# Gate pieces as three rounded products, and ScalarE taking the gate selection and the inner row rounding of the expert turns

## What is computed

```
# mixer: the gates of the merge are a projection of h, 3 x 1024 columns wide
g_merge = (h @ w_in + b_in)[:, -3 * 1024:]
gm = sigmoid(g_merge.reshape(B, S, 3, 1024))
merged = gm[:, :, 0] * (o_a @ w_branch[0]) + gm[:, :, 1] * (o_b @ w_branch[1]) + gm[:, :, 2] * (o_c @ w_branch[2])

# experts: each token goes to 4 of 32, weighted by the softmax of their logits
gate = softmax(top_v)
hb = xb @ w1[e] + b1[e];  g, u = hb[:, :1024], hb[:, 1024:]
g = minimum(g, 7.0);  u = clip(u, -7.0, 7.0)
y = ((u + 1.0) * g * sigmoid(1.702 * g)) @ w2[e] + b2[e]
out = zeros.at[row_tok].add(y * row_w[:, None])
```

## Time and profile before

| | |
|---|---|
| median of three runs | 2846.25 us (2841.96 to 2849.76) |
| profiled execution, its own time | 2838.52 us |
| its span | 2836.7 us |
| TensorE busy | 2732.5 us, 96% |
| VectorE busy | 2101.5 us, 74% |
| ScalarE busy | 1516.0 us, 53% |
| read from HBM | 773 MB, 273 GB/s over the span |

### The profile page before, as it was taken

One profiled execution on the slowest core, in us unless ns is written; L12 is line 12 of the kernel. 1 busy time (PEld: TensorE's weight loads), 2 busy tenths in 40 slices (PEclk: granted clock), 3 DMA queues, 4 the chain that ended last, 5 costly groups with the idle time before them and its releaser, 6 DMA issues. The chain is left out here.

```text
span 2836.7 us, 43415 instructions
## 1 busy us (share of the span) xinstructions
PE 2732.5 (96%) x17490; PEld 2458.2 (87%) x17490; DVE 2101.5 (74%) x1854; ACT 1516.0 (53%) x1296; POOL 0.4 (0%) x6
## 2 busy tenths in 40 slices
PE   6999999999999999999998999999989999999998
PEld 5888888877787877778776999999979999999998
DVE  6335549999999999999998888676446766754453
ACT  0033318888888888888884443343444444432342
POOL 0000000000000000000000000000000000000000
PEclk9999999999999999999998999999999999999999
DMA  9753438999999999999995876777417767754551
GB/s 392 262 178 126 153 125 354 378 369 381 382 383 385 381 385 383 383 383 385 364 382 209 282 271 248 252 255 258 156 60 252 276 224 260 273 171 164 163 188 66
DMA packets 172689, 776.08 MB, mean 274 GB/s; under 512 B 12272, under 2 KB 38000, under 8 KB 121616
## 3 DMA queue, kind: packets, MB, share of 16 engines
q1 hardware_dynamic: 168640, 768.71, 71.5%
q10 hardware_dynamic: 3920, 5.49, 0.7%
HBM read 773.10 MB, written 1.05 MB: 273 GB/s over the span
## 5 line engine op out<-in xcount | busy, mean ns | idle before, releaser
L2271 DVE TENSOR_TENSOR w_low<-ring,w_high 128x2048 fp32r<-128x2048 f32 x396 | 880.6, 2285 | 16.3 <-DVE arena L2322 7.1
L901 ACT ACTIVATE w_high<-ring 128x2048 fp32r<-128x2048 f32 x396 | 734.6, 1906 | 75.4 <-PE psum L1564 75.3
L2411 DVE TENSOR_TENSOR w_low<-ring,w_high 128x2048 fp32r<-128x2048 f32 (+1 forms) x199 | 432.8, 2184 | 326.9 <-ACT w_high L1019 324.0
L1019 ACT ACTIVATE w_high<-ring 128x2048 fp32r<-128x2048 f32 (+1 forms) x199 | 362.4, 1829 | 567.6 <-PE psum L1204 489.2
L1204 PE MATMUL psum<-h_high,w_high 128*128 128x256 f32 x2080 | 591.4, 284 | 21.6 <-ACT h_high L1032 20.2
L1204 PE MATMUL psum<-h_high,w_low 128*128 128x256 f32 x2080 | 593.5, 285 | 0.0
L1204 PE MATMUL psum<-h_low,w_high 128*128 128x256 f32 x2080 | 591.1, 286 | 0.0
L1204 PEld LDWEIGHTS psum<-h_high,w_high 128*128 128x128 f32 x2080 | 402.7, 194 | 23.9 <-issue 22.1
L1204 PEld LDWEIGHTS psum<-h_low,w_high 128*128 128x128 f32 x2080 | 397.7, 192 | 0.0
L1204 PEld LDWEIGHTS psum<-h_high,w_low 128*128 128x128 f32 x2080 | 396.7, 191 | 0.0
L1564 PE MATMUL psum<-w_low,xg 128*128 128x512 f32 x1056 | 294.4, 400 | 4.1 <-DVE w_low L2271 2.9
(11 more groups left out here) (278 smaller groups left out, 3226.3 us busy)
## 6 DMA issues: line engine op xcount, KB each, us to landing
ring<-in_exp_w SPq DMA_DIRECT2D x396, 1024.0 KB, 8.3
ring<-in_ffn_w SPq DMA_DIRECT2D x135, 1024.0 KB, 5.2
ring<-in_mod_w SPq DMA_DIRECT2D x96, 1024.0 KB, 5.6
ring<-in_ffn_w SPq DMA_DIRECT2D x40, 768.0 KB, 4.8
ring<-in_w_in SPq DMA_DIRECT2D x24, 1024.0 KB, 10.7
ring<-in_even_w_in SPq DMA_DIRECT2D x12, 1024.0 KB, 7.2
ring<-in_conv_w_in SPq DMA_DIRECT2D x12, 1024.0 KB, 5.1
ring<-in_w_branch SPq DMA_DIRECT2D x6, 1024.0 KB, 5.1
```

The source lines that it names most:

```text
L901: act.activation(high_ap(j, D), slot_ap(PLAN.moe_slot + j), ACT.Copy).then_inc(sem("expert_high_ready" + c.x), 1)
L1019: act.activation(high_ap(m, cols), slot_ap(s, 2, cols), ACT.Copy).then_inc(sem("w_high_ready"), 1)
L2271: dve.tensor_tensor(low_ap(PLAN.moe_slot + j, D), slot_ap(PLAN.moe_slot + j), high_ap(j, D).bitcast(F32), ALU.subtract).then_inc(sem("expe ...
L2411: dve.tensor_tensor(low_ap(s, cols), slot_ap(s, 2, cols), high_ap(m, cols).bitcast(F32), ALU.subtract).then_inc(sem("w_split"), 1)
```

## The change

Three things change.

1. **Gate pieces.** Each of the twelve pieces is made of three products of split operands (`split_piece`). ScalarE rounds h once (`h1_high`, in the arena) and each piece's weights (`high_piece`, into ring places 7 and 8 in turn); VectorE makes the low part of h in place over `hT`, behind the last z piece, and each piece's low part in place over its slot (`low_piece`). Piece n+1 is prepared in step s of piece n: on ScalarE behind the exponentials of step s+1, on VectorE behind step s's modulation slots. The ring has seven places instead of nine from there to the experts; two small buffers move into ring place 11.
2. **Gate selection.** `selG` is made by ScalarE (`gated`): four activations of 128 x (2 x 64) with a scale read per partition, ahead of (first pair) or behind the copy of gather half 0. `select` on VectorE keeps only the comparison, without a wait, and signals `sel_ready` behind it.
3. **Inner rows.** The rounding of the inner rows is done by ScalarE (`hidden_rounded`): of expert 0 behind high part 17, of expert 1 behind the row copy of the down product of expert 0. VectorE issues the hidden product without waiting, does one low part in between (slot 16, or slot 20), waits for the rounding, and subtracts.

```diff
+            act.activation(h1_high[:, :, :], hT[:, :, :], ACT.Copy).then_inc(sem("h1_high_ready"), 1)
@@ ScalarE, attention steps
+            def high_piece(n):
+                s = PLAN.slots[f"mpiece{n}"]
+                if n < 2:
+                    await_release(act, PLAN.piece_before[n])
+                else:
+                    await_unit(act, U[f"mpiece{n - 2}"])
+                await_slot(act, s)
+                act.activation(piece_parts(n)[0], slot_ap(s, DC, 2 * P), ACT.Copy).then_inc(sem("piece_high_ready"), 1)
+            high_piece(0)
             for s in range(len(ATT)):
                 turned(s)
                 if s + 1 < len(ATT):
                     exps(s + 1)
+                if s in PIECE_STEPS and s != PIECE_STEPS[-1]:
+                    high_piece(PIECE_STEPS.index(s) + 1)
@@ ScalarE, expert turns
+            def gated(gate_of):
+                for b in range(TB):
+                    for e in range(2):
+                        chosen = sel[:, b, e, :].bitcast(F32)[:, None, :].broadcast_to([P, 2, CAP])
+                        act.activation(selG[:, b, e, :, :], chosen, ACT.Copy, scale=gate_of(580 + COLS_E * b + e))
+                def hidden_rounded(e):
+                    act.wait_ge(sem("hidden_whole" + c.x), c.turn * 2 + (e + 1))
+                    act.activation(hid[e][:, :, 0, :], moe_buf("up").rearrange("p (k s) -> p k s", k=DC),
+                                   ACT.Copy).then_inc(sem("hidden_high" + c.x), 1)
-                high(c, 15, 16, 17, 18)
+                high(c, 15, 16, 17)
+                hidden_rounded(0)
+                high(c, 18)
...
                 rows("down0", "y_rows0", 1.0 / ALPHA)
+                hidden_rounded(1)
                 c.await_unit(act, "gather0")
                 gathered(0, c.unit("gather0"), c.x)
+                gated(lambda at: small[:, bass.ds(c.columns + (at + 2), 1)])
                 high(c, 23)
@@ TensorE
+            def split_piece(n):
+                ...
+                pe.wait_ge(sem("piece_split"), n + 1)
+                wh, wl = piece_parts(n)
+                for k in range(DC):
+                    for j in range(2):
+                        dst, cols = unit(u)[:, j * T:(j + 1) * T], slice(j * P, (j + 1) * P)
+                        pe.matmul(dst, wh[:, k, cols], h1_high[:, k, :], start=(k == 0 and j == 0), stop=False, ...)
+                        pe.matmul(dst, wh[:, k, cols], h_low[:, k, :], start=False, stop=False, ...)
+                        mm = pe.matmul(dst, wl[:, k, cols], h1_high[:, k, :], start=False, stop=(k == DC - 1), ...)
@@ VectorE, attention steps
+            await_unit(dve, U["zpiece3"])
+            dve.wait_ge(sem("h1_high_ready"), 1)
+            dve.tensor_tensor(h_low[:, :, :], hT[:, :, :], h1_high[:, :, :].bitcast(F32), ALU.subtract)...
+            low_piece(0)
             soft(1)
...
                 for i in range(*ATT_MOD_SLOTS[s:s + 2]):
                     mod_slot(20 + i)
+                if s in PIECE_STEPS and s != PIECE_STEPS[-1]:
+                    low_piece(PIECE_STEPS.index(s) + 1)
                 if s == SUBLN_STEP:
                     subln_mean()
                 if s == SUBLN_STEP + 2:
                     subln_scale()
@@ VectorE, expert turns
-                    steps.link(dve.scalar_tensor_tensor(ub, ub, 1.0, glu, ALU.add, ALU.mult))
-                    steps.link(dve.tensor_scalar(hid[e][:, :, 0, :], ub, 1.0, None, ALU.mult))
+                    dve.scalar_tensor_tensor(ub, ub, 1.0, glu, ALU.add, ALU.mult).then_inc(sem("hidden_whole" + c.x), 1)
+                    low(c, *between)
+                    dve.wait_ge(sem("hidden_high" + c.x), c.turn * 2 + (e + 1))
                     dve.tensor_tensor(hid[e][:, :, 1, :], ub, hid[e][:, :, 0, :].bitcast(F32), ALU.subtract)...
-                up_half(0)
-                low(c, 16, 17, 18)
+                up_half(0, 16)
+                low(c, 17, 18)
...
-                up_half(1)
-                low(c, 20, 21, 22, 23)
+                up_half(1, 20)
+                low(c, 21, 22, 23)
```

More of the change, by code:

```diff
@@ L41 @@
 Z_PIECES = [8, 10, 12, 14]
-RING, RING1 = 12, 9
+RING, RING1, RING_ATT = 12, 9, 7
 SLOT = 2 * D
@@ L238, in make_plan @@
     p.piece("zpiece3", 14)
+    p.placed()
+    p.piece_before = [p.holder[at] for at in range(RING_ATT, RING1)]
+    p.places, p.next = RING_ATT, p.next % RING_ATT
     p.unit("cmp_turn", 2)
@@ L272, in make_plan @@
     p.placed()
+    for n in (10, 11):
+        p.holder[RING_ATT + n % 2] = p.slots[f"mpiece{n}"]
     p.high_before = [p.holder[at] for at in range(RING2, RING1)]
@@ L471, in build @@
         cmpP = area(14336, TB * 8, 16)
-        cmpPT, hidden_rows = area(11264, 2048), area(11264, 2, 2 * P)
+        cmpPT = ring[:, RING - 1, :]
+        hidden_rows = ring[:, RING - 1, 0:4 * P].rearrange("p (m c) -> p m c", m=2)
         gm = ring[:, RING1:RING, :].rearrange("p s (c t) -> p (s c) t", t=T)
@@ L981, in _ @@
                 await_unit(act, U["gather"] + half)
+                if half == 0:
+                    gated(first_gate)
                 gathered(half, unit(U["gather"] + half), "")
@@ L1454, in compressed @@
                 mm.then_inc(psum_full, 1)
+            def split_piece(n):
+                u = U[f"mpiece{n}"]
+                open_unit(pe, u)
+                if n == 0:
+                    pe.wait_ge(sem("h1_low_ready"), 1)
+                pe.wait_ge(sem("piece_split"), n + 1)
[3 more added lines that the diff above has]
+                        dst, cols = unit(u)[:, j * T:(j + 1) * T], slice(j * P, (j + 1) * P)
+                        pe.matmul(dst, wh[:, k, cols], h1_high[:, k, :], start=(k == 0 and j == 0), stop=False,
+                                  skip_group_check=True)
+                        pe.matmul(dst, wh[:, k, cols], h_low[:, k, :], start=False, stop=False, skip_group_check=True)
+                        mm = pe.matmul(dst, wl[:, k, cols], h1_high[:, k, :], start=False, stop=(k == DC - 1),
+                                       skip_group_check=True)
+                mm.then_inc(psum_full, 1)
             for n in range(len(Z_PIECES)):
@@ L1465, in _ @@
                 if s in PIECE_STEPS:
-                    piece(f"mpiece{PIECE_STEPS.index(s)}")
+                    split_piece(PIECE_STEPS.index(s))
                 if s:
@@ L2039, in _, with low_piece @@
             last.then_inc(sem("cmp_probs"), 1)
+            def low_piece(n):
+                s = PLAN.slots[f"mpiece{n}"]
+                dve.wait_ge(sem("piece_high_ready"), n + 1)
+                high, low_ = piece_parts(n)
+                dve.tensor_tensor(low_, slot_ap(s, DC, 2 * P), high.bitcast(F32), ALU.subtract).then_inc(
+                    sem("piece_split"), 1)
+            await_unit(dve, U["zpiece3"])
+            dve.wait_ge(sem("h1_high_ready"), 1)
+            dve.tensor_tensor(h_low[:, :, :], hT[:, :, :], h1_high[:, :, :].bitcast(F32), ALU.subtract).then_inc(
+                sem("h1_low_ready"), 1)
+            low_piece(0)
             soft(1)
@@ L2242, in _, with select @@
             slot_no = const("iota")[:, 0:CAP]
-            def select(pair_of, x, done):
+            def select(pair_of, x):
                 slots = slot_no[:, None, :].broadcast_to([P, 2, CAP])
@@ L2249, in select @@
                     last = dve.tensor_tensor(sel[:, b, :, :], slots, of, ALU.is_equal)
-                done(last)
-                for b in range(TB):
-                    of = pair_of(580 + COLS_E * b)[:, :, None].broadcast_to([P, 2, CAP])
-                    for d in range(2):
-                        last = dve.tensor_tensor(selG[:, b, :, d, :], sel[:, b, :, :].bitcast(F32), of, ALU.mult)
                 last.then_inc(sem("sel_ready" + x), 1)
@@ L2258, in first_pair @@
                 return small[:, at:at + 2]
-            select(first_pair, "", link)
+            select(first_pair, "")
             find_busiest()
@@ L2363, in _ @@
             with dve.Fori(0, PAIRS) as i:
-                steps.enter(i, 7)
+                steps.enter(i, 2)
                 experts(first_turn(i), steps)
@@ L2393, in later @@
                     steps_x.n = 0
-                    steps_x.enter(c.turn, 7)
+                    steps_x.enter(c.turn, 2)
                     experts(c, steps_x, last)
```

18 lines of the change are left out of this document (12 added, 6 removed).

## The result

The changed kernel takes 2820.89 us (median of 4 runs, 2813.6 to 2824.23), the kernel before in the same session 2844.62. The ratio is 0.9907, with a 95% interval of 0.9894 to 0.9919: 26 us less, where 33 were forecast. In a later session the same two kernels stood at 0.9885 (0.9868 to 0.9902), 33 us. The profiled execution of after took 2813.6 us, with a span of 2811.8.

A forecast was written before the change was run, and what follows sets the result against it. VectorE was taken to bound the expert turns, TensorE the attention and FFN. Turns -23.2, single turn and first gather -0.5, attention -9.5 make -33 us: 2805.5 on the profiled execution, median 2813, range 2800 to 2831.

The forecast's parts named there:

- The turns: Expert turns: a loop of hand-overs through the engines sets the period, 64.7 us, saving 1.45 a turn, 23 in sixteen.
- VectorE's floor: Expert turns: shortest period VectorE's own load allows, 66.17 less 2.0, so 64.2 us.
- rival A: Expert turns reach the limit of VectorE's load, 9 us more gain: 2804 us; chance 0.13.
- ScalarE's margins: Expert turns: the two inner roundings end 1.5 and 0.8 us before their covering low parts, so they cost nothing.
- D: Rival: second inner rounding waits behind ScalarE's down-product copy, delaying VectorE and TensorE; slower, 2861 us at 3.5 lateness; chance 0.05.
- B: Rival: a ScalarE link uses up the 0.8 us margin, turns gain only 0.5 us each: 2828 us; chance 0.14.
- The single turn: Turn with one expert: nothing lies between its hidden product and rounding, a loss of about 0.3 us.
- The first gather: Start of the expert turns: no wait for the gate products any more, gaining at most 0.90 us.
- The gate pieces: Attention: twelve pieces fall from 6.78 to 5.66 us, 1.12 each; stretch -9.5 us, bounds -14 and +2.
- Step 10: Attention: low part 9 goes straight into the path ahead of softmax, +2.2 us, and that step's 1.12 gain is swallowed.
- rival C: Attention gains nothing, as low parts delay softmax in several steps, not one: 2823 us; chance 0.08.
- The base: Starting time: the profiled execution's 2838.5 us lay 7.7 under the median of three, 2846.25, so 2805.5 became 2813.

The follow-up runs named there:

- the swishes later: Each ScalarE swish one high part later, on after with the last high part ahead of the second gather's copy and heads scaled a step later: 2795.56 us, 0.9814.
- the later scaling: Against after, VectorE scales the attention's difference heads one step later: ratio to before 0.9883.
- low part 16 behind: Against after, low part 16 goes back behind the hidden low part, both roundings staying on ScalarE: ratio to before 0.9914.

## Why the prediction was right

The forecast was 2813 us, the measured medians are 2821 and 2814 in two sessions.

- **The turns, 23 us.** Right in its mechanism and in the size of the undisturbed turn: 64.7 forecast, 64.73 in thirteen of fifteen. By its steps: from the end of the second gather to the end of the last next low part 5.3 us forecast, 759.61 - 754.28 = 5.3 measured; from there round to the first load with the hidden product 41.0, measured 795.27 - 754.28 = 41.0 (795.27 is the next first load, in the weight loads of after above); from that load to the next gather's end 23.6, measured 754.28 - 730.54 = 23.7. TensorE's wait for the hidden low part: 1.4 forecast, 22.9 / 16 = 1.43. The term that was too large is the gain itself, 23.2 instead of 16 x 1.24 = 19.8 us: the disturbed turns weren't in the sum. The lower clock was weighed for the gap of the attention and not for this one, though the wait of 1.4 us was forecast beside it.
- **VectorE's floor, 64.2.** This step failed without touching the forecast. With the swishes later the turn takes 63.67, and 0.5 us of VectorE's waiting is still in it, so its own load is at most 63.2. I took the 66.17 us for full of load; but 14.9 us of idle time, 0.9 a turn, stand in the earlier trace rows, and I quoted them as small and then left them in. So rival A's 2804 wasn't the bottom, and the distance between the loop and the floor was 1.5 us, not 0.4.
- **ScalarE's margins** of 1.5 and 0.8 us: the first rounding ends at 728.3 and its cover, low part 16, at 729.8; the second at 741.8 and low part 20 at 742.7. Margins of 1.5 and 0.9. The forecast named a wait of VectorE for a rounding as a sign that it is wrong, and there are two, 0.9 us together, both for the second rounding and both in the two turns at the lower clock (0.53 us at 547.5 and 0.39 at 807.8). There TensorE's down product is late and ScalarE's copy and the rounding behind it too: this is D's path, but it doesn't start on its own. In the other thirteen periods B's and D's premise didn't come about. The four gate products took 1.26 us instead of 1.5. The estimate that the prediction drew from the Trainium skill ("ScalarE: Activation LUTs", What ACT_TABLE_LOAD costs) was 0.386 us each. It left out what the same section of the Trainium skill says next, that activations back to back overlap by some 93 ns: with it the estimate is 0.386 + 3 x 0.293 = 1.27 us, and the trace agrees.
- **The single turn**: its hidden low part starts 22.5 us behind the additions instead of 22.3; VectorE waits 0.69 us there for the rounding. Forecast was a loss of 0.3.
- **The first gather**: its 0.75 us of waiting went, and 0.75 came back ahead of the first turn's loads, since ScalarE makes the four products ahead of the copy. Nothing, where 0.2 was allowed.
- **The gate pieces.** 5.66 us each as forecast, at full clock. The ten distances between pieces other than 8 to 9 shrank from 12.59 to 11.49 in the mean (1.10, forecast 1.12). Step 10 (piece 8 to 9) grew from 17.9 to 18.7 and 19.4 us, by the means of the profiles in the table from 17.8 to 19.3; the forecast's sum had +2.2 for it and 0.5 for the clock, so this term was too large by 1.2. TensorE's gap at step 11 was put at 4.6 us and was 2.5 and 3.7. In the first profile the piece ahead of it ran 8.2 us at a mean clock of 0.67; that its lateness hid part of the low part is my reading, no run shows it. Against this stands what the forecast didn't have: it named idle time that vanishes before softmax in other steps as a sign of being wrong, and it vanished in two, from 3.0 to 0 and from 7.0 to 0.2 us. That is rival C, in small: from piece 6 to piece 8 the six new profiles of the table take 22.5 us in the mean, the old ones 23.4, and 21.2 were forecast. The mean start of piece 11 is 318.0 in the five old profiles and 310.0 in the six new ones of the table: 8.0 us, and 1.1 for the last piece itself, 9.1 against the 9.5 forecast. The nearness is in part luck. From piece 0 to piece 11 the gain is 9.8 us (144.1 to 134.3), and piece 0 starts 1.8 us later in the mean, with the clock as told above. Behind piece 11 some is lost again: the first load of the expert turns stands at 437.6 us in the mean of the old profiles and at 430.7 in that of the new, 6.9 us. That fits the time, by which the pieces alone give 6.8 (4.0 to 9.7). Where those 2 us go was not looked into.
- **The base.** 2838.5 was a favourable execution: 171 at piece 0, where the thirteen others have 173.6 to 177.9. I carried its 7.7 us under the median over as a whole; the later profiles bear that out.

So of the 7 us between 33 and 26, some 3 are the turns at the lower clock; for the rest, the second session's 33 shows that it is within what the sessions differ by.

## What to carry to other kernels

When two engines look equally full, count the chain of hand-overs round the loop as well as the load of each, and take the idle time that the groups list out of the load first. A part that gives its full amount alone can give less with another beside it: then look for the wait that is new, and move the work in front of it (here two swishes, one high part and one scaling, worth another 20 us by the ratios, 0.9885 to 0.9814). A wait of the matrix engine costs its length and sometimes the clock behind it. How often can't be told from its length (1.1 us did it more often here than 1.4), so count the disturbed periods one by one. And look for signs of being wrong that came in small, even where the sum came out.

## What the runs showed of the hardware

- A wait of 1.4 us ahead of TensorE's loads, once a turn, was followed by some 3 us at the lower of the two clock levels in two and three turns of fifteen in the two profiles of after, in one each with the turns only and the roundings only, and in two with the later scaling: 9 of 75. A wait of 1.1 us was in five and in four, 9 of 30; one of 0.7 us in none of 15. With a wait of 1.6 us behind the first hidden loads instead of ahead of them, there were none either: 90 periods of six profiles (before twice, the gate pieces only, the gate products only, expert 0 rounded by VectorE, low part 16 behind). The Trainium skill ("TensorE: Matmul & The Clock Gate", HAM oscillation) says that gaps between bursts of matmuls bring the low clock back; the trace agrees in part: gaps were followed by it and the shortest wasn't, but 1.1 us was more often than 1.4, and 1.6 at another place never.
- The clock fell at about 170 us in all fourteen profiles, and in seven of them once before, at about 155 to 160, with TensorE's busy time full (30.0 of 30 us from 150 to 180, where the ends of matmuls are modelled), in the same code of TensorE. With it piece 0 starts up to 7 us apart (170.8 to 177.9). The pair of before and after alone shows 3.9 us for the gate pieces at piece 11, where the means of eleven profiles show 8.0.
- The copy with a pointer for its scale takes 0.32 us for 128 x 128 elements in a row of four on ScalarE, and 0.22 as a product on VectorE.
